# The down product of a feed-forward layer by seven quarter products instead of eight

## The reference

```python
h = rms_norm(x, g_pre_mix) * (1 + sc1) + sh1
...                                   # token mixers on h @ w_in, then
x = x + gt1 * rms_norm(mix @ w_out, g_post_mix)
h = rms_norm(x, g_pre_ffn) * (1 + sc2) + sh2
u = depthwise_conv3(h @ w_up) + conv_b          # (2048, 2 * 2816)
gate, val = split(u, 2)
y = (gelu(gate) * val) @ w_down                 # (2048, 2816) @ (2816, 1024)
x = x + gt2 * rms_norm(y, g_post_ffn)
```

## Time and profile before

| | |
|---|---|
| time, median of 3 runs | 2241.74 us (2240.74 to 2243.68) |
| profiled execution, first to last instruction | 2239.4 us |
| TensorE matmul busy | 2199.2 us, 98% |
| VectorE, ScalarE, GpSimd busy | 1211.5, 749.2, 225.7 us |
| bytes moved | 476.98 MB |

### The profile page before, as it was taken

The page is one execution under the profiler, slowest core; times in us unless marked ns, Lnnn a source line. Parts: engine busy times, 40 slices in busy tenths (PEclk is TensorE's granted clock), DMA queues, the critical chain, the costliest instruction groups (busy, mean ns, idle before and its releaser), DMA issues.

```text
span 2239.4 us, 36245 instructions
## 1 busy us (share of the span) xinstructions
PE 2199.2 (98%) x13099; PEld 1774.1 (79%) x13099; DVE 1211.5 (54%) x2154; ACT 749.2 (33%) x1521; POOL 225.7 (10%) x150
## 2 busy tenths in 40 slices
PE   7999999999999999999999999999999999999998
PEld 4776788888887778888888778888888877888886
DVE  3567683856767564252555845244354665515244
ACT  3555533343445331111235542122024444212012
POOL 2322344444200000000000000000000000000000
PEclk9999999999999999999999999999999999999999
DMA  9965688887663456555564345655546344555554
GB/s 366 400 235 188 225 319 320 288 293 277 238 237 115 171 186 226 194 200 188 179 232 154 138 148 207 239 190 189 197 166 239 132 169 150 206 191 199 192 189 149
DMA packets 114442, 476.98 MB, mean 213 GB/s; under 512 B 7935, under 2 KB 38921, under 8 KB 69257
## 3 DMA queue, kind: packets, MB, share of 16 engines
q1 hardware_dynamic: 114313, 475.24, 58.5%
HBM read 372.45 MB, written 102.76 MB: 212 GB/s over the span
## 4 chain that ended last, share of the span: by engine, by line
PE 88%; DVE 5%; issue 3%; ACT 2%; DMA 2%; DVEq 0%; SPq 0%; POOL 0%; ACTq 0%; POOLq 0%
PE ps L614 17%; PE ps L616 16%; PE ps L615 16%; PE ps L639 9%; PE ps L641 9%; PE ps L640 9%; PE ps L716 1%; PE ps L1026 1%; PE ps L1029 1%; PE ps L1027 1%; PE ps L566 1%; DVE cv L1885 1%; PE ps L763 1%; DMA raw<-in_w_in_dram 1%; PE ps L884 1%
## 5 line engine op out<-in xcount | busy, mean ns | idle before, releaser
L614 PE MATMUL ps<-hTh,wt 128*128 128x512 f32 x1792 | 707.8, 395 | 2.3 <-DVE hTl L1566 2.0
L616 PE MATMUL ps<-hTh,wt 128*128 128x512 f32 x1792 | 698.4, 390 | 0.0
L615 PE MATMUL ps<-hTl,wt 128*128 128x512 f32 x1792 | 698.2, 390 | 0.0
L614 PEld LDWEIGHTS ps<-hTh,wt 128*128 128x128 f32 x1792 | 336.4, 188 | 81.2 <-issue 13.0
L616 PEld LDWEIGHTS ps<-hTh,wt 128*128 128x128 f32 x1792 | 336.5, 188 | 71.1
L615 PEld LDWEIGHTS ps<-hTl,wt 128*128 128x128 f32 x1792 | 336.7, 188 | 66.9
L1883 DVE TENSOR_SCALAR cv<-ub,CW 128x512 f32<-128x512 f32 x176 | 101.1, 575 | 462.8 <-ACT ub L1426 448.6
L1426 ACT ACTIVATE ub<-ps 128x512 f32<-128x512 f32 x176 | 105.2, 598 | 680.1 <-PE ps L616 630.9
L639 PE MATMUL ps<-wt,pTh 128*128 128x512 f32 x692 | 270.4, 391 | 0.3 <-ACT wt L1082 0.3
L641 PE MATMUL ps<-wt,pTh 128*128 128x512 f32 x692 | 269.4, 389 | 0.0
L640 PE MATMUL ps<-wt,pTl 128*128 128x512 f32 x692 | 269.3, 389 | 0.0
(11 more groups left out here) (280 smaller groups left out, 2354.2 us busy)
## 6 DMA issues: line engine op xcount, KB each, us to landing
wt<-split_w SPq DMA_DIRECT2D x264, 1024.0 KB, 4.8
split_w<-wt SPq DMA_DIRECT2D x88, 1024.0 KB, 7.1
raw<-in_w_up_dram SPq DMA_DIRECT2D x22, 1024.0 KB, 10.2
XT<-in_w_ada_dram SPq DMA_DIRECT2D x10, 1024.0 KB, 11.6
XN<-in_x_dram SPq DMA_DIRECT2D x4, 2048.0 KB, 9.6
raw<-in_w_in_dram SPq DMA_DIRECT2D x8, 1024.0 KB, 15.1
XR<-in_x_dram SPq DMA_DIRECT2D x4, 2048.0 KB, 9.7
raw<-in_w_down_dram SPq DMA_DIRECT2D x8, 1024.0 KB, 9.2
```

Of the source, the lines that this page charges most:

```text
L614: mm(ps[:, bank, :], w, hTh[:, k, :], start=(k == 0), stop=False)
L615: mm(ps[:, bank, :], w, hTl[:, k, :], start=False, stop=False)
L616: ins = mm(ps[:, bank, :], wl[:, slot, k, :], hTh[:, k, :], start=False, stop=(k == KD - 1))
```

## The change

The down product of a group is done by a scheme of Strassen's kind. The group's hidden values are cut in four by token half (256 tokens) and by even and odd 128-channel tile, w_down in four by the same channel tiles and by column half. Seven products of quarters (P0 to P6 here, `q` in the code) replace eight. Three of them have a plain quarter of w_down, four (q = 2, 3, 5, 6) have a sum of quarters, T1 to T4. Four of the left operands are sums as well.

- **Groups.** One step, then five groups of two steps (`NS`). The down product of group f-1 stands on TensorE behind the first two up units of group f; the last one stands alone at the end of the block (`last_down`).
- **TensorE.** A product of a two-step group is 2 token tiles by 2 channel tiles by 3 matmuls. P3, P5 and P6 are added in PSUM onto what P0, P3, P5 left there, and P4 onto P2, and each is read out in between, so TensorE waits in `down_piece` until the earlier result has been taken by `evacuate`.
- **VectorE.** A step gets four additions of 128 by 256 (`token_half_sums`), and the low parts cover seven instead of four tiles of 256 columns. Each product is added to Y, 14 additions a group; in the first group ScalarE copies four of the seven. VectorE's program order is: the step before with its low parts, `conv(0)`, `conv(1)`, then the 14 additions, then `conv(2)`.
- **GpSimd, block 0.** Beside the low parts it forms the four sums T of each group (`differ`), in the order low P0, T1, low P1, low P2, T3, T2, low P3, T4, low P4, P5, P6.
- **GpSimd and ScalarE, blocks 1 to 3.** The sums are kept unsplit (`keep_sum`), fetched (`fetch_sum`), and split again in each block: one ScalarE rounding and one GpSimd low part for each of 24 units.
- **Last down product of a block.** The transposes and splits for the next block are spread between P2 and P6.
- **Loops.** Blocks and steps are written out.

```diff
-FH = (8, 8, 6)
-J0 = (0, 8, 16)
-DN_K = (((0, 1), (2, 3), (4, 5), (6, 7)),) * 2 + (((0, 1), (2,), (3, 4), (5,)),)
+NS = (1, 2, 2, 2, 2, 2)
+NF = len(NS)
+SPLIT_FIRST = (4, 5)
+PRODUCTS = ("A11 B11", "A12 B21", "S1 T1", "S2 T2", "S4 B22", "S3 T3", "A22 T4")
+LEFT = (0, 2, 3, 4, 6, 5, 1)
+BANK = (4, 6, 2, 4, 2, 4, 4)
+DEST = ((2, 0), (2, 0), (0, 1), (2, 1), (2, 1), (0, 1), (0, 0))
+T_OF = {2: 0, 3: 1, 5: 2, 6: 3}
+COPIES, ADDS = (0, 2, 3, 6), (1, 4, 5)
...
 @block.gpsimd
+            def differ(f, out_, a, c, width_):
+                at = lambda r: quarter_of(f, r, True)[:, 0:width_]
+                pool.tensor_tensor(at(out_), at(a), at(c), ALU.subtract).then_inc(s["t_added"], 1)
...
+            for n in range(RING, UNITS):
+                pool.wait_ge(s["unit_done"], n - RING + 1)
+                low(n)
...
+                if q == 0 and n == LAST_UNIT[f, q]:
...
+                    differ(f, 0, 2, 0, w)
+                if q == 2:
...
+                    differ(f, 2, 3, 2, w)
...
+                    differ(f, 0, 3, 0, w)
+                if q == 3:
...
+                    differ(f, 1, 1, 0, w)
+            for b in range(1, NB):
+                for f in range(NF):
+                    for n, (g, j) in SUM_UNIT.items():
+                        if g == f:
+                            low(n, False, (b - 1) * SUMS + (UNITS + 4 * f + j - n))
 @block.tensor
+                def down_piece(f, q, k, n, t, at):
+                    pe.wait_ge(s["p_ready"], b * (2 * STEPS) + (2 * (ST0[f] + k) + (1 if LEFT[q] < 3 else 2)))
+                    if k == 0:
+                        if q < 2 and f == 0:
+                            pe.wait_ge(s["t32_ready"], tb + 12)
+                        elif q == 2:
+                            pe.wait_ge(s["acc_taken"], eb_ + (E_IN + 4 * (ST0[f] + NS[f] - 1) + 2 + t + 1))
+                        else:
+                            name, count = evac(b, *((f - 1, 6), (f - 1, 1), None, (f, 0), (f, 2), (f, 3), (f, 5))[q], t)
+                            pe.wait_ge(s[name], count)
...
+                    mm(ps[:, bank, :], h, w_hi_, start=(k == 0 and q < 3), stop=False, skip_group_check=True)
...
+                for f in range(1, NF):
+                    up_units(f, 0, (0, 1))
+                    for q, ks, n in DN_UNITS[f - 1]:
+                        down_unit(f - 1, q, ks, n)
+                    up_units(f, 0, (2, 3))
+                    up_units(f, 1, range(4))
+                last_down()
 @block.vector
+                    def token_half_sums():
+                        a21, a11, a22, a12, s1, s2, s3, s4 = (P32[:, j, :] for j in range(8))
+                        dve.wait_ge(s["prod_ready"], jb + 2)
+                        up(tt(s1, a21, a22, ALU.add))
+                        up(tt(s3, a11, a21, ALU.subtract))
+                        up(tt(s2, s1, a11, ALU.subtract))
+                        tt(s4, a12, s2, ALU.subtract).then_inc(s["sums_ready"], 1)
...
+                    conv(0)
+                    conv(1)
+                    if f and i == 0:
+                        down(f - 1)
...
+                    conv(2)
+                    gated(0)
+                    conv(3)
+                    gated(1)
+                    token_half_sums()
+                    hidden_low(0)
+                    hidden_low(1)
```

More of the change, by code:

```diff
@@ new lines @@
+UP_UNIT, DN_UNITS, UNITS = sequence()
+assert UNITS % RING == 0
+UP_OF = {n: key for key, n in UP_UNIT.items()}
+DN_OF = {n: (f, q, ks) for f in range(NF) for q, ks, n in DN_UNITS[f]}
+LAST_UNIT = {(f, q): n for f in range(NF) for q, ks, n in DN_UNITS[f]}
+SUM_UNIT = {n: (f, T_OF[q]) for n, (f, q, ks) in DN_OF.items() if q in T_OF}
+RANK = tuple(sum(m % RING == n % RING and m not in SUM_UNIT for m in range(n)) for n in range(UNITS))
+PER_SLOT = tuple(sum(m % RING == v and m not in SUM_UNIT for m in range(UNITS)) for v in range(RING))
@@ L72, in ada_use @@
     return slot, sum(s == slot for p in ADA_SLOT[:e] for s in p) + 1
[L74 to L84, removed]
+ACT_STEPS, DVE_STEPS, UP_STEPS = 28, 76, 19
 class Steps:
@@ L450, in later_block @@
                 load_x(b)
[L451 to L461, removed]
+                for n in range(OFF_OUT + RING, UNITS):
+                    if n not in SUM_UNIT:
+                        refill(n)
+                    if n in UP_OF:
+                        f, i, u = UP_OF[n]
+                        if i == NS[f] - 1:
+                            sp.wait_ge(s["w_lo"], (b - 1) * SUMS + (UNITS + 4 * f + u - 3))
+                            fetch_sum(f, u)
+                        if f == NF - 1 and i == 0 and u == 2 and not last:
+                            load_next(b)
                 for u in range(0 if last else RING):
@@ L467, in _ @@
             first_block()
-            with sp.Fori(1, NB - 1) as b:
+            for b in range(1, NB - 1):
                 later_block(b, False)
@@ L1499, in _ @@
             one_block(0, True)
-            with act.Fori(1, NB - 1) as b:
+            for b in range(1, NB - 1):
                 one_block(b, False)
@@ new lines, in down @@
+                def down(f):
+                    for q in range(7):
+                        if f == 0 and q in COPIES:
+                            continue
+                        if last and f == NF - 1 and q == 6:
+                            for i in range(2):
+                                finished(i, slice(0, D))
+                        for t in range(2):
+                            evacuate(f, q, t)
+                        if f == NF - 1 and not last:
+                            for k in ((), (0, 1), (2,), (3, 4), (5, 6), (7,), ())[q]:
+                                split(12 + k, k)
@@ L1943, in _ @@
             one_block(0, True)
-            with dve.Fori(1, NB - 1) as b:
+            for b in range(1, NB - 1):
                 one_block(b, False)
```

678 lines of the change are left out of this document (391 added, 287 removed).

## The result

The changed kernel takes 2311.91 us (median of 4 runs, 2310.21 to 2315.36), the kernel before 2241.97 us beside it: 1.0316 times, interval [1.0303, 1.0328]. The forecast of 2348 us had the sign and most of the cause; a net loss of 106 us was forecast and 70 came.

The account below looks back on a forecast made before the run. TensorE's matmul count was taken to bound the kernel: -59.9 (matmuls) + 1.4 (tail) + 107 (block 0) + 36 (blocks 1, 2) + 9 (block 3) + 13 (clock) = +106.5, giving 2348 us; range 2248 to 2395.

Parts of the forecast that it names:

- the tail: Kernel end, after P6: VectorE has 6.9 us of instructions left, then the same 3.1 us as today; +1.4 us.
- rival of a stretched VectorE staying in its slack: Block 0: few held instructions, costing 10 us there; kernel faster at 2207 us; chance 0.15.
- Transfers: Block 0 feed-forward: a 290 GB/s limit makes it 10% longer, +20 us on the forecast, 2368 us; chance 0.06.
- at one VectorE instruction for each: Block 0 full phases: VectorE finishes one instruction per GpSimd instruction, so P0's addition comes at +26 us, P3 18 late.
- GpSimd busy from P0 to P6: Block 0 product phases: expected sign that GpSimd works throughout, with eight instructions in a row taking 21 us.
- block 0, four full phases: Block 0, phases inside the block: P3 waits 17 us for VectorE's addition of P0 in each; +68 us.
- first phase: Block 0, group 0, with half-width instructions: a bit over half of 17 us, +10 (3 to 14).
- last phase: Block 0's end: the 12 us of blocks 1 and 2 plus 11 GpSimd instructions by 1.54 us; +29 (16 to 31).
- blocks 1 and 2, each: Late VectorE in the last phase and held instructions in five other phases: 18 us a block (14 to 25).
- clock: Whole kernel: the forecast sum's allowance for TensorE's slower clock, +13 us.
- the five inner phases of blocks 1 and 2: Four GpSimd instructions each hold VectorE 1.5 us, conv(1) has about 4 to spare: 0 to 2.5 each, 6 together.
- rival of GpSimd's chain alone: GpSimd's own excess of 7.4 us sets the waits: block 0 35 us, kernel 2252 us; chance 0.10.

Follow-up runs that it names:

- the last runs: Kernel before, block 0 low parts of up units computed twice on GpSimd, 2306.89 us; or the same time added as writes of zeros, 2273.59 us.
- that run: Changed kernel with ScalarE making convolution edges, additions first, T3 earlier, and sums kept in DRAM as high and low parts: 2287.08 us, 1.0202.

## Why the prediction came out as it did

**What held.** The pace of 0.2267 us and the 264 matmuls; the tail, +1.5 us for +1.4; the mechanism, GpSimd's run of reads stretching VectorE (1218 and 1664 ns for 752) until the addition of P0 is late; the order of the blocks. The rival of a stretched VectorE staying in its slack needed less than 2.3 us a phase; it was 9 to 11. Transfers did not bind in block 0 of the changed kernel: its share is 0.67, and ScalarE waited 18.1 us for raw up weights there, no more than the 22.3 us of the kernel before.

**The step that was mis-sized** is "at one VectorE instruction for each", +26 us to the addition, in block 0's full phases. Its premise was eight GpSimd instructions in a row. But GpSimd has gaps, because its low parts wait for ScalarE, which waits for the sums and for VectorE: it stood idle for 10.60 us until 430.29, 4 us after P0 began, so the sign "GpSimd busy from P0 to P6" did not come. In the timeline above the ten convolution instructions took from 429.88 to 444.95, 15.1 us, only five of them held, and three short ones slipped into one gap. The addition ended 19.3 us after P0 began, not 26. Term by term:

| term | forecast | waits measured |
|---|---|---|
| block 0, four full phases | 68 | 42.9 (1.6 + 9.5 three times, 2.3 + 7.3) |
| first phase | 10 | 11.3 |
| last phase | 29 | 23.5 |
| blocks 1 and 2, each | 18 | 10.6 and 10.7 |
| block 3 | 9 | 5.9 |
| clock | 13 | 20.7 |

Of the 36 us by which the forecast was too high the full phases make 25 and blocks 1 and 2 make 15; the clock, too low by 8, hides part of that. The waits of block 0 hold another 3.2 us in short intervals.

**A second wrong step** is the 6 us a block for the five inner phases of blocks 1 and 2: TensorE waits there for under 1 us. Four GpSimd instructions spread over a group leave conv(1) in time. The last phase was forecast at 12 and measured at 9.8 and 10.4. With short low parts 3.9 and 4.7 us of these waits stayed, put down here to VectorE's queue of additions and splits, which no run took away; the rest went with the low parts, 6.5 and 6.7 us a block with the clock.

**The clock.** No run shows the 13 us that the forecast's sum has for the clock; what the runs showed in its place is 20.7 us, 7.7 more. In block 0 TensorE ran at half pace beside nine waits; those beside the waits of 3.1, 5.9 and 4.6 us cost 4.9 us together. The one in the last phase of block 1 cost 1.7 us. Timeline and stretch:

```profile
1208.80 0.47 PE L1177 MATMUL ps<-wt,pTh 128*128 128x512 f32 x1 [4.30 <-DVE pTl L2127]
...
1209.81 0.63 PE L1178 MATMUL ps<-wt,pTl 128*128 128x512 f32 x1
1210.23 0.63 PE L1179 MATMUL ps<-wt,pTh 128*128 128x512 f32 x1
```

```profile
1209.60:1213.10 3.50, 3.50 (x10) 2.80 (x9) 2.51 (x4) 1.56 (x3) 2.46 (x1) 0.52 0.31 87
```

**The rival of GpSimd's chain alone**, 2252 us, is near what writes in place of reads give, 2240 us. It is a true part of the loss, at most the 34.7 us that stayed in block 0, and the holding by reads stands on top of it. That its 35 us for block 0 met the 34.7 is in part luck, as VectorE's new work and the holding by writes are in the measured number.

**Still open.** How much of the 34.7 us is GpSimd's chain, how much VectorE's additions and sums and how much the holding by writes was not separated. Nor was a version tried with eight products in block 0 and seven in the later ones. From the table its blocks 1 to 3 would give 1.6, 0.4 and 6.3 us less the 1.5 of the tail, some 7 us in 2242, if the sums of quarters could be made in block 0 for nothing; the last runs say that block 0 has no such room.

## What to carry to other kernels

Removing work from the engine that binds is worth its pace only while the others' work for it fits in the shorter time: here the 15 us saved in block 0 cost 102 us more of GpSimd. Before adding GpSimd work that reads SBUF, count part of it as VectorE's too: for the same instructions VectorE was busy 120 us longer in block 0, beside 260 us of GpSimd, than in block 1, beside 56. An order changed or an instruction cut in two mostly moves the wait (8 and 5 us came back of 70). When a wait's named releaser was long done, look up what each condition's last event was.

## What the runs showed of the hardware

- In block 0 of the changed kernel VectorE's convolution instructions with two SBUF operands were held by GpSimd instructions that read (up to 2922 ns for 752); in the run with writes only they were not held at all (at most 755 ns). One-operand ones were held by writes too: a 128 by 2 copy took 160 to 164 ns beside no GpSimd instruction and up to 948 beside writes.
- Removing 88 short instructions, many of them held, freed 16 us, as the next instruction was held instead.
- Behind a wait of 4.3 us the granted clock was 0.52 in the 3.5 us that began 0.8 us after its end; the pace there was 0.4267 us a matmul, for 0.2267 at a granted clock of 1.00.
- Fetches reached 417 GB/s over 19 us with a share of 1.01, and in block 1 of that run TensorE waited for fetches six times, 1.1 us at most.
